# Start addresses of the feed-forward's split operands, block by block

## What is computed

```python
h = rmsnorm(x, norm_ffn[i])
gt, up = jnp.split(h @ w_ffn_in[i], 2, axis=-1)
x = x + (jax.nn.silu(gt) * up) @ w_ffn_out[i]
```

## Time and profile before

| | |
|---|---|
| time, median of 3 runs | 2138.44 us (2137.98 to 2140.2) |
| the profiled execution | 2139.59 us, of which the span from first to last instruction is 2137.8 |
| TensorE busy | 2113.5 us (99%), 18652 matmuls |
| VectorE, ScalarE, GpSimd busy | 1640.1 us (77%), 1195.2 (56%), 58.5 (3%) |
| mean granted TensorE clock | 0.997 |
| HBM read | 381.53 MB |

### The profile page before, as it was taken

How to read it: one execution, slowest core, us unless ns; L and a number is a source line. 1 busy time by engine, 2 the same in 40 slices (tenths; PEclk the granted TensorE clock), 3 DMA queues, 4 the chain that set the end, 5 groups by cost and what they waited for, 6 DMA issues and landing times.

```text
span 2137.8 us, 47790 instructions
## 1 busy us (share of the span) xinstructions
PE 2113.5 (99%) x18652; PEld 2055.5 (96%) x18652; DVE 1640.1 (77%) x2620; ACT 1195.2 (56%) x1803; POOL 58.5 (3%) x54
## 2 busy tenths in 40 slices
PE   9999999999999999999999999999999999999998
PEld 8999999999999999899999999999899999999998
DVE  8987877987877776778957877776678947877764
ACT  6646644565555445546648745445446658845443
POOL 0000000000000000000002200000000002200000
PEclk9999999999999999999999999999999999999999
DMA  7434655654446556554455566556554556565553
GB/s 251 159 128 141 204 190 186 195 171 142 151 157 215 190 189 206 187 168 158 161 190 191 167 203 208 186 187 213 185 169 148 169 183 193 174 201 186 187 189 127
DMA packets 109984, 385.00 MB, mean 180 GB/s; under 512 B 12480, under 2 KB 16768, under 8 KB 109312
## 3 DMA queue, kind: packets, MB, share of 16 engines
q1 hardware_dynamic: 101664, 368.66, 52.2%
q10 hardware_dynamic: 8160, 14.04, 2.1%
HBM read 381.53 MB, written 1.11 MB: 179 GB/s over the span
## 4 chain that ended last, share of the span: by engine, by line
PE 89%; DVE 6%; ACT 2%; issue 2%; DMA 0%; DVEq 0%; ACTq 0%
PE acc L777 25%; PE acc L779 24%; PE acc L778 24%; DVE w_lo L1811 2%; PE acc L896 1%; PE acc L897 1%; PE acc L898 1%; PE acc L841 1%; PE acc L843 1%; PE acc L842 1%; ACT w_hi L1310 1%; PE mid L1133 1%; PE mid L1214 1%; DVE pr L2564 0%; PE mid L964 0%
## 5 line engine op out<-in xcount | busy, mean ns | idle before, releaser
L1811 DVE TENSOR_TENSOR w_lo<-w_raw,w_hi 128x1024 fp32r<-128x1024 f32 x694 | 848.5, 1227 | 306.8 <-ACT w_hi L1310 297.9
L1310 ACT CAST w_hi<-w_raw 128x1024 fp32r<-128x1024 f32 x694 | 724.7, 1047 | 541.3 <-PE acc L779 473.5
L777 PE MATMUL acc<-h_hi,w_hi 128*128 128x256 f32 x2096 | 599.4, 286 | 0.3 <-DVE w_lo L1811 0.3
L779 PE MATMUL acc<-h_hi,w_lo 128*128 128x256 f32 x2096 | 587.5, 280 | 0.0
L778 PE MATMUL acc<-h_lo,w_hi 128*128 128x256 f32 x2096 | 586.3, 280 | 0.0
L777 PE MATMUL acc<-g_hi,w_hi 128*128 128x256 f32 x1456 | 410.0, 282 | 0.8 <-DVE w_lo L1811 0.7
L779 PE MATMUL acc<-g_hi,w_lo 128*128 128x256 f32 x1456 | 407.2, 280 | 0.0
L778 PE MATMUL acc<-g_lo,w_hi 128*128 128x256 f32 x1456 | 406.8, 279 | 0.0
L777 PEld LDWEIGHTS acc<-h_hi,w_hi 128*128 128x128 f32 x2096 | 395.7, 189 | 7.7 <-issue 5.7
L779 PEld LDWEIGHTS acc<-h_hi,w_lo 128*128 128x128 f32 x2096 | 396.1, 189 | 0.0
L778 PEld LDWEIGHTS acc<-h_lo,w_hi 128*128 128x128 f32 x2096 | 395.1, 188 | 0.5
(11 more groups left out here) (434 smaller groups left out, 3394.3 us busy)
## 6 DMA issues: line engine op xcount, KB each, us to landing
w_raw<-weights_d SPq DMA_DIRECT2D x695, 512.0 KB, 3.9
even<-rows_d ACTq DMA_DIRECT2D x16, 256.0 KB, 4.3
odd<-rows_d ACTq DMA_DIRECT2D x32, 128.0 KB, 3.4
p<-p_d ACTq DMA_DIRECT2D x3, 1080.0 KB, 8.5
rdec<-decay_d ACTq DMA_DIRECT2D x2, 768.0 KB, 5.3
p<-p_d SPq DMA_DIRECT2D x1, 1024.0 KB, 10.7
out_d<-work SPq DMA_DIRECT2D x4, 256.0 KB, 2.3
x_all<-x_d SPq DMA_DIRECT2D x1, 516.0 KB, 4.3
```

What stands on the lines that cost most here:

```text
L777: mm(dst, wh, hi[:, k, :], start=first and j == 0, stop=False)
L779: done = mm(dst, wl, hi[:, k, :], start=False, stop=last and j == len(ks) - 1)
L1310: nc.scalar.copy(w_hi[:, slot, :], w_raw[:, slot, :]).then_inc(hi_done, 1)
L1811: tt(w_lo[:, slot, :], w_raw[:, slot, :], w_hi[:, slot, :].bitcast(F32), SUB).then_inc(lo_v, 1)
```

## The change

The blocks of `f_hi` and `f_lo` are set 1040 bytes apart (256 floats and 4 unused), those of `g_hi` and `g_lo` 1056 bytes (256 and 8 unused). The starts of `f_hi` and `g_hi` stay; `f_lo` and `g_lo` move up to make room, and `f_act`, `f_prod`, `ptmp` and `tiny` with them. No instruction, wait, loop or transfer is added or taken away.

```diff
-        f_hi = in_arena("f_hi", 288, [P, FF, T], F32R, lead=4)
-        f_lo = in_arena("f_lo", 320 + 4 * FF * T, [P, FF, T], F32R, lead=4)
-        f_act = in_arena("f_act", 46144, [P, 2, T])
-        f_prod = in_arena("f_prod", 48192, [P, 2, T])
-        g_hi = in_arena("g_hi", 52512, [P, KD, T], F32R, lead=4)
-        g_lo = in_arena("g_lo", 52544 + 4 * KD * T, [P, KD, T], F32R, lead=4)
+        f_hi = in_arena("f_hi", 288, [P, FF, T + 4], F32R, lead=4)[:, :, 0:T]
+        f_lo = in_arena("f_lo", 23360, [P, FF, T + 4], F32R, lead=4)[:, :, 0:T]
+        f_act = in_arena("f_act", 46336, [P, 2, T])
+        f_prod = in_arena("f_prod", 48384, [P, 2, T])
+        g_hi = in_arena("g_hi", 52512, [P, KD, T + 8], F32R, lead=4)[:, :, 0:T]
+        g_lo = in_arena("g_lo", 61248, [P, KD, T + 8], F32R, lead=4)[:, :, 0:T]
@@
-        ptmp = in_arena("ptmp", 46144, [P, 2, PAIRS * PC])
-        tiny = in_arena("tiny", 50240, [P, 32, PAIRS])
+        ptmp = in_arena("ptmp", 46272, [P, 2, PAIRS * PC])
+        tiny = in_arena("tiny", 50400, [P, 32, PAIRS])
```

## The result

Over 12 runs each the kernel now takes 2141.16 us (2139.42 to 2143.2) against 2138.44 before (2135.66 to 2140.2). The ratio is 1.0016, with a 95% interval from 1.0009 to 1.0024: slower by 0.16%, some 3.4 us (the two medians themselves are 2.7 us apart). That is inside the 0.2% that I called no change and inside my range, but it is slower beyond the interval, where I had forecast 0.4 us faster.

A forecast was written before the change was run, and what follows sets the result against it. TensorE, busy 99% of the span, was taken as the bound. Small gains at L822 and in f's blocks, all else 0, summed to -0.4 us: median 2138.0 us from 2138.44, own range 2134.2 to 2142.7, chance 0.52.

The forecast's parts named there:

- the second reading, the rhythm: Multiplying by g and f: longest chain pieces recur every 1.76 us, 15 matmuls, taken as a fixed-rate supply, not addresses.
- term (1): The 4368 g matmuls in the common order: change 0, by the rhythm and the equal pitches.
- The first reading: Runs by h, s, m and f: pitch equal to 0.02 ns, so the 256-byte steps separating them change nothing.
- The third reading: Make-up of a pitch: 112.0 ns per 256 columns, leaving 5.3 ns once a matmul, start address included.
- (2): The 48 matmuls of L822: 2.7 ns less each if equal neighbours are their trouble, 0.13 us gained.
- (3): f blocks at multiples of 32: 1056 matmuls at 0.3 ns, 0.3 us gained, not beyond rounding.
- (4): Next block's start after L779, 2160 matmuls: bounds 0 and 2.9 us gained, taken as 0.
- (5): VectorE's writing of the parts, two-block writes over a gap included: 0.3 us lost at most, taken as 0.
- The slower rival: Moving blocks of g and f meet weights at other distances: 5208 matmuls pay 2.7 ns, 14.1 us, 2152.5; chance 0.22.
- The faster rival: Staggered g and f blocks lose some of the 5.3 ns once-only part: half is 17.6 us, 2120.9; chance 0.26.
- The rule on lines: SBUF blocks: 16-byte lines with a crossing penalty; every block still covers 64 lines, so the sum is 0.

The follow-up runs named there:

- e4_range: Bench of matmuls alone: moving block at 64 places by 1024 for two weights places, then six block steps; 117.34 ns at step 1024, 118.03 at 1056.
- e9_narrow: Bench of matmuls alone: moving block at 16 places, with 128 or 32 weights columns, plain float32, or 512 moving columns; means 118.8, 115.1, 215.8 (a record), 230.0 ns.
- the grid: Bench of matmuls alone: 64 pairs of moving and weights remainders by 128, blocks 1024 bytes apart; 113.3 to 123.2 ns a matmul.
- e2_f_only: Kernel before with only f's blocks set 1040 bytes apart and the scratch tensors moved; 2138.57 us, ratio 1.0002.
- The map: Bench of matmuls alone in three-part order: moving blocks at the kernel's remainders, weights in 256 places; 115.6 to 122.2 ns, mean 117.9.
- e6: Kernel before with only g's blocks set 1152 bytes apart; 2136.44 us against 2138.13, ratio 0.9989.
- e7: Kernel before with the split weights moved to remainders 16 and 48 by 256 (from 208 and 240), front memory reordered; 2117.99 us against 2138.13, ratio 0.9905.

## Why the prediction was wrong

**The step that failed** is the second reading, the rhythm, and with it term (1) of the sum: "The 4368 g matmuls in the common order: 0". I read 15 matmuls as a supply with a rate of its own because 15 fits neither 24 nor 66. But when every block and every weights piece has the same remainder, the addresses give no loop of 24 to come back after: the three matmuls of every block meet the same three distances, and 15 is five times three (why five, no run shows). As soon as the blocks differ, the rhythm is the loop's: 72 matmuls, three slabs of g. The term measured 0.73 ns a matmul, 3.0 us in the four g stages, instead of 0.

**The first reading** was right and I wrote down its limit: equal pitch of h, s and m shows that 256-byte moves are free, and e4_range confirms a period of exactly 256. It said nothing of the change.

**The third reading** bounded the wrong thing. I took 112 ns for each 256 columns as a fixed rate and 5.3 ns as all that a start could touch. In e9_narrow 512 columns take 226.7 to 233.3 ns by place, and 256 take 113.3 to 123.3: a place changes more than 5.3 ns. The float32 row, my nearest for starts at a multiple of 32, comes from a form that no place affects (215.8 ns at all 16), so it could not tell. I also misread it: a float32 matmul makes two records, here as in L1118 (four records for two matmuls), so 215 ns is half a matmul and the 5 ns are a record's, not a matmul's.

**Terms (2) to (5).** L822: 0.13 us expected, 0.96 us became 0.95 for eight; equal neighbours were the wrong reason, the distance of 96 (by 256) to the weights is the right one, 119.9 ns in the grid too. (3) and (4) have no basis left; f as a whole moved by 0.13 ns, 0.28 us. (5), writes and waits at 0, held: e2_f_only shows the moved scratch free, VectorE's busy time in the g windows is the same within 0.2 us, and the two-block writes across the gap take 684 ns instead of 686 (L2354).

**The slower rival was the right mechanism**, blocks that fall on other distances from the weights, at 0.22. Its price was mis-sized: I charged every changed distance with L822's 2.7 ns, 14.1 us in all. The map's mean over all places is 117.9, only 0.6 above the kernel's own place, so a walk through many remainders costs about that: 0.6 x 6624 = 4.0 us, an estimate from the bench; 3.5 measured (3.0 in the g stages, 0.3 in those by f, and the rest in the last two layers' first 16 slabs, where g is stationary: from their first start to the mixing part's they take 48.52 and 47.46 us instead of 48.36 and 47.32). That the two sums agree is partly luck: the same 0.6 ns would charge the f blocks 1.3 us, where they pay 0.3, and g 2.7, where its four stages alone pay 3.0. Its sign, a pitch that depends on k, came true (116.7 to 121.4 ns by block of g), but its rule did not: by it three blocks of g in four would each have paid 2.7 ns, while block 3 pays 4.1, block 7 1.4, and none of the others more than 1. Its condition, that it counts from 0.8 ns on, was not reached. That my time lay only 3 us off is luck too: a block's matmuls get up to 2 ns shorter or 4.3 longer, and my 0 came near only because most of that cancels, nearly all of it in f.

**The faster rival** did not occur here, but e6 and e7 show that such a gain exists; it lies in the choice of distances, not in variety.

**The rule on lines.** The Trainium skill ("SBUF — State Buffer", Specifications (TRN2)) has 16-byte lines, and by it the sum was 0. Steps of 1040, 1056 and 1152 are whole lines all three and gave 117.9 to 118.0, 118.0 and 116.7 to 116.8 ns against 117.3. The line's size, whatever it is, is not what decides here.

**Still open** is the mechanism under the table: why the period is 256 bytes, why weights at a multiple of 32 and 16 past one have different values, how three matmuls with three distances combine, and why a difference of 64 has two values. I have tables, not a model. The mixing parts of the first two layers also differ by up to 1.6 us between executions of nearly equal kernels, at any layout, so there a single profile can't tell a gain of a microsecond.

## What to carry to other kernels

When matmuls stream at full rate with a load of weights for each, operand addresses are a tuning parameter, worth 1% of this kernel's time, with 115.6 to 122.2 ns between the best and the worst place of the map: measure the pitch over the weights' place by 256 in a bench (all 256 places took 2217 us), then move the one tensor that all matmuls share. Making addresses varied earned about the mean over the map with most steps tried, which is worse than a good fixed place. And a row of another operand type or rate is no bound for this one: look for the property that the change moves, and if every row of before has the same value of it, say that the trace is silent and widen the range, not narrow it by a pattern.

## What the runs showed of the hardware that I had not expected

An fp32r matmul of 256 columns with its 128x128 weights costs 113.3 to 123.3 ns by the difference of its operands' addresses, at a granted clock of 1.00 throughout. The pattern repeats every 256 bytes and vanishes for plain float32 (215.8 ns a record at 16 of 16 places). It does not need the other engines: the bench at the kernel's own place has 117.34 ns, the kernel 117.33 in the f stage. Moving the two weights tensors gave 20 us of 2138 with no instruction added or taken away.
